# A two-layer hybrid transformer block on one core: one weight split moved by a step, the last scatter placed before the branch, and gated linear attention taken by pairs of heads

## What is computed

```python
def gla_chunked(q, k, v, glog, s0):
    g = cumsum(glog, within each chunk of 64); g_last, g_mid = ...
    att = einsum(q * exp(g - g_mid), k * exp(g_mid - g))
    att = where(tril, att, 0)
    o_intra = einsum(att, v)
    ds = einsum(k * exp(g_last - g), v); decay = exp(g_last)
    s_prev = scan over chunks: s <- decay * s + ds
    o_inter = einsum(q * exp(g), s_prev)
    return o_intra + o_inter

def gla_bidir(...):                       # both directions, summed
    return o_f + flip(o_b)

def moe_ffn(h, router, w1, w3, w2):
    combine = softmax over the 2 best experts of each token
    for e in 8 experts:
        out += combine[:, e] * ((silu(h @ w1[e]) * (h @ w3[e])) @ w2[e])
```

## Time and profile before

| | us |
|---|---|
| runs before, three | 1795.90, 1798.19, 1801.63 |
| median | 1798.19 |
| the profiled execution, its own time | 1800.37 |
| its span, first to last instruction | 1798.4 |
| TensorE busy | 1694.8 (94%) |
| VectorE busy | 1015.4 (56%) |
| ScalarE busy | 794.1 (44%) |
| data read | 404.7 MB |

### The profile page before, as it was taken

How to read it: one execution, slowest core, us unless ns; L and a number is a source line. 1 busy time by engine, 2 the same in 40 slices (tenths; PEclk the granted TensorE clock), 3 DMA queues, 4 the chain that set the end, 5 groups by cost and what they waited for, 6 DMA issues and landing times.

```text
span 1798.4 us, 25945 instructions
## 1 busy us (share of the span) xinstructions
PE 1694.8 (94%) x10337; PEld 1310.9 (73%) x10337; DVE 1015.4 (56%) x1403; ACT 794.1 (44%) x1225; POOL 55.0 (3%) x40
## 2 busy tenths in 40 slices
PE   6999989999999999999887999999999998889886
PEld 4877668988888888887677887777788887444442
DVE  3335656677677434643766986667799895101012
ACT  4416545622212223725546765556677774100101
POOL 0000000000000000000000530000000000000000
PEclk8999989999999999999978999999999999999998
DMA  8412053244467422231024977668999897899997
GB/s 332 150 71 71 1 201 145 79 185 170 185 237 263 179 94 94 80 117 48 24 71 151 357 287 258 237 235 354 344 351 360 343 360 295 327 421 421 420 421 327
DMA packets 56830, 407.53 MB, mean 227 GB/s; under 512 B 6322, under 2 KB 6450, under 8 KB 7808
## 3 DMA queue, kind: packets, MB, share of 16 engines
q1 hardware_dynamic: 56128, 404.38, 58.6%
q0 software_dynamic: 288, 0.79, 0.1%
q10 hardware_dynamic: 288, 0.63, 0.1%
HBM read 404.73 MB, written 1.05 MB: 226 GB/s over the span
## 4 chain that ended last, share of the span: by engine, by line
PE 82%; DMA 7%; DVE 5%; ACT 4%; issue 2%; SPq 0%; POOL 0%; DVEq 0%; ACTq 0%
PE psum L2243 60%; PE psum L2850 4%; DMA raw_more<-units 4%; DMA raw<-units 4%; PE psum L2860 2%; PE psum L2748 2%; PE psum L2806 1%; PE psum L2876 1%; PE psum L2888 1%; PE psum L2442 1%; PE psum L2269 1%; DVE w_lo L1551 1%; PE psum L2466 1%; PE psum L2538 1%; PE psum L2260 1%
## 5 line engine op out<-in xcount | busy, mean ns | idle before, releaser
L1551 DVE TENSOR_TENSOR w_lo<-raw,w_hi 128x1024 fp32r<-128x1024 f32 x130 | 153.0, 1220 | 144.9 <-ACT w_hi L980 144.6
L2243 PE MATMUL psum<-act_hi,w_hi 128*128 128x512 f32 (+1 forms) x608 | 221.1, 364 | 2.1 <-DVE w_lo L1551 2.1
L2243 PE MATMUL psum<-act_hi,w_lo 128*128 128x512 f32 (+1 forms) x608 | 218.7, 360 | 0.0
L2243 PE MATMUL psum<-act_lo,w_hi 128*128 128x512 f32 (+1 forms) x608 | 218.7, 360 | 0.0
L980 ACT ACTIVATE w_hi<-raw 128x1024 fp32r<-128x1024 f32 x130 | 130.3, 1053 | 161.8 <-DMA raw<-units 87.5
L2018 DVE TENSOR_TENSOR w_lo<-raw,w_hi 128x2048 fp32r<-128x2048 f32 x75 | 171.5, 2289 | 41.7 <-ACT w_hi L1360 41.4
L1360 ACT ACTIVATE w_hi<-raw 128x2048 fp32r<-128x2048 f32 x75 | 143.8, 1918 | 68.4 <-PE psum L2243 43.2
L2018 DVE TENSOR_TENSOR w_lo<-raw_more,w_hi 128x2048 fp32r<-128x2048 f32 x49 | 112.1, 2289 | 46.2 <-ACT w_hi L1360 46.0
L2243 PE MATMUL psum<-w_hi,act_hi 128*128 128x256 f32 (+1 forms) x368 | 130.2, 354 | 3.4 <-DVE w_lo L1551 1.7
L2243 PE MATMUL psum<-w_hi,xt_hi 128*128 128x512 f32 x332 | 132.1, 398 | 0.0
L2243 PE MATMUL psum<-w_lo,xt_hi 128*128 128x512 f32 x332 | 129.9, 391 | 0.0
(11 more groups left out here) (363 smaller groups left out, 3249.3 us busy)
## 6 DMA issues: line engine op xcount, KB each, us to landing
raw<-units SPq DMA_DIRECT2D x275, 1024.0 KB, 5.1
raw_more<-units SPq DMA_DIRECT2D x107, 1024.0 KB, 6.7
X<-ctx_in SPq DMA_DIRECT2D x1, 1024.0 KB, 8.5
X<-x_in SPq DMA_DIRECT2D x1, 1024.0 KB, 10.6
out<-X SPq DMA_DIRECT2D x2, 512.0 KB, 2.8
const<-const_in ACTq DMA_DIRECT2D x1, 524.0 KB, 7.4
rope<-rope_in POOLq DMA_DIRECT2D x2, 256.0 KB, 4.9
wsm<-wsm_in SPq DMA_DIRECT2D x1, 384.0 KB, 7.0
```

The costliest lines, as they stand in the source:

```text
L1551: ins = dve.tensor_tensor(w_lo[:, w_slot(i), part], raw[:, i % RING, part], w_hi[:, w_slot(i), part].bitcast(F32), ALU.subtract)
L2243: ins = pe.matmul(dst, lhs(a), rhs(b), start=first and n == 0, stop=last and n == 2)
```

## The change

Three edits.

1. The split of the last split unit (`LATE_SPLIT`, `down` of chunk 54) is taken out of `split_behind` and done by ScalarE and VectorE in step 55, behind the silu of chunk 55 and the turned columns of chunk 54.
2. TensorE's scatter of pass 7 stands before its branch (and no longer in pass 8's steps if there is one), each of the four scatters in a bank of its own with no wait for the additions before it. ScalarE's copy of the output moves behind its branch, and behind the load of the square-root table.
3. GLA goes by (pair of heads, token tile): 8 items in layer 0 and 4 in layer 1. VectorE makes two masked copies and adds the two directions into `Am_sum`; TensorE then needs one 128x128 matmul for each head where it had four of half width, and goes round the four 64x64 quadrants of its array in `M` and in the state products. `KT` and `DS` of the second pair, the scans, the products, the head sums and the splits of the output units get new places. In layer 0 the two scans are put in two items (2 and 3) and `OG` of an item stands before `DS`. In layer 1 the factors of the second pair (`gate_differences`, `gate_exps`) move forward into attention, and only one of the two output units is split by VectorE within GLA.

```diff
-SUBS_IN = {0: {4: 0, 5: 2, 16: 1}, 1: {2: 0, 3: 2, 8: 1}}
-EXPS_IN = {0: {5: 0, 6: 2}, 1: {3: 0, 4: 2}}
+SUBS_IN = {0: {4: 0, 5: 2, 16: 1}, 1: {2: 0, 3: 2, 6: 1, 7: 3}}
+EXPS_IN = {0: {5: 0, 6: 2}, 1: {3: 0, 4: 2, 7: 1, 8: 3}}
+LATE_SUBS, LATE_EXPS = {0: (3,), 1: ()}, {0: (1, 3), 1: ()}
...
+SCANS = {0: {2: (1,), 3: (3,)}, 1: {1: (1, 3)}}
...
     s = SPLIT_OF[UNIT_AT[key]] + W_RING
-    return [s] if s < split_limit(r) else []
+    return [s] if s < split_limit(r) and s != LATE_SPLIT else []
...
+LATE_SPLIT = SPLIT_OF[UNIT_AT["down", NARROW[0] * FC - 1]]
... ScalarE, gla
-                key = ("OG", l, i)
-                wait_filled(act, key)
-                act.activation(og[:, t, h * P:(h + 1) * P], bank(key)[:, 0:P], ACT.Copy)
...
+                rows_copied(2 * i + 2)
+                wait_filled(act, ("OG", l, i, 1))
+                for hh in range(2):
+                    key, h = ("OG", l, i, hh), 2 * pair + hh
+                    act.activation(og[:, t, h * P:(h + 1) * P], bank(key)[:, 0:P], ACT.Copy)
...
+                rows_copied(2 * i + 3)
... ScalarE and VectorE, run: behind the split of step g
+                if up == NARROW[0] * FC:
+                    high(LATE_SPLIT)
...
-            output(RUNS[r][-1])
...
             act.activation(std[:, 0:1], eps, ACT.Sqrt).then_inc(sem("root_table"), 1)
+            output(p)
... VectorE, gla
+            for i, (pair, t) in enumerate(gla_items(l)):
+                wait_filled(dve, ("M", l, i, 1))
...
+                for h in range(2):
+                    ins = dve.copy_predicated(Am[:, h, :, :].rearrange("p d n -> p (d n)"), tri.bitcast(I32),
+                                              bank(("M", l, i, h))[:, 0:2 * P])
...
+                empties(dve.tensor_tensor(Am_sum[:, i % 2, :, :], Am[:, :, 0, :], Am[:, :, 1, :], ALU.add), ("M", l, i, 0))
+                for dp in SCANS[l].get(i, ()):
+                    scan(l, dp)
+                for key in beside_gla(l, 2 * i) + beside_gla(l, 2 * i + 1):
+                    if key[0] == "modx":
+                        mod_step(*key)
                 if i in LOW_IN_GLA[l]:
                     split_upto(out_unit(l, LOW_IN_GLA[l][i]))
... TensorE, gla
+                for h in range(2):
+                    wait_emptied(pe, ("OG", l, i, h))
+                    pe.matmul(bank(("OG", l, i, h))[:, 0:P], Am_sum[:, i % 2, h, :], gv[:, t, (2 * pair + h) * P:(2 * pair + h + 1) * P],
+                              start=True, stop=False, skip_group_check=True)
...
+                if i < len(items):
+                    masked_scores(i)
                 if i == TURNS_AT[l]:
                     keys_turned(l, PAIR_ORDER[2:])
+                for key in beside_gla(l, 2 * i):
                     mod_step(*key)
                 if i >= 1:
+                    outputs(i - 1)
+                if i == TURNS_AT[l]:
+                    state_steps(l, PAIR_ORDER[2:])
+                for key in beside_gla(l, 2 * i + 1):
+                    mod_step(*key)
... TensorE, scatter and the end
-            before = 4 * p + (n if bank_of == SCATTER_BANK else 0)
+            before = 4 * p + (n if p != RUNS[-1][-1] and p + 1 not in RUN_STARTS else 0)
...
+            finish(RUNS[k][-1])
             with pe.If(run_valid(pe, k)):
...
-            with pe.Else():
-                finish(EXPERTS + k - 1)
```

More of the change, by code:

```diff
@@ L318 @@
 UNIT_AT = {key: m for m, key in enumerate(UNIT_LIST)}
+RUN_STARTS = tuple(passes[0] for passes in RUNS)
 RUN_END = tuple((passes[-1] + 1) * EXPERT_UNITS for passes in RUNS)
@@ L2502, in gla, with masked_scores @@
             items = gla_items(l)
+            quadrants = ((0, 0), (1, 1), (0, 1), (1, 0))
+            rows_of = lambda n: slice(n * CHUNK, (n + 1) * CHUNK)
+            def masked_scores(i):
+                pair, t = items[i]
+                pe.wait_ge(sem(f"gmul{l}"), 8 * (pair + 1))
+                for h in range(2):
+                    wait_emptied(pe, ("M", l, i, h))
+                for d in range(2):
+                    for n, (h, half) in enumerate(quadrants):
+                        r, c = rows_of(h), rows_of(2 * t + half)
+                        ins = pe.matmul(bank(("M", l, i, h))[rows_of(half), d * P + half * CHUNK:d * P + (half + 1) * CHUNK],
+                                        factors(l, 1, 2 * d + pair)[r, c], factors(l, 0, 2 * d + pair)[r, c], start=True, stop=True)
+                        if d == 1 and n >= 2:
+                            ins.then_inc(filled, 1)
```

165 lines of the change are left out of this document (75 added, 90 removed).

## The result

| | before | changed |
|---|---|---|
| median of 7 runs, us | 1801.63 | 1786.29 |
| range, us | 1795.9 to 1808.81 | 1784.65 to 1793.15 |
| ratio, with its 95% interval | 1 | 0.9918 (0.9891 to 0.9945) |
| profiled execution, us | 1800.37 | 1784.65 |
| its span, us | 1798.4 | 1782.8 |

One execution of the kernel before, beside the second group of experiments, took 3338.81 us and is left out of the ratios; all others are of one kind.

What follows compares the result with a forecast made beforehand. No single limit: DMA in the 64-slot passes, chains of short handovers at the end and in both GLAs. Terms -8.7 - 2.3 - 8.6 + 5 = -14.6 us gave a median of 1783.6, range 1774.5 to 1790.5.

Steps and rivals of the forecast that it cites:

- A, the seam: In the 64-slot passes: splitting `down` 54 one step later removes the dry DMA gap; -8.7 us (-7.5 to -9.2).
- B, the end: Behind the last `down`: scatters before TensorE's branch, ScalarE branching early, bring the last addition sooner; -2.3 us (-0.5 to -5).
- C, layer 1 with attention: Layer 1's GLA: last product starts sooner, though exponentials push attention's end by 0.7 us; -8.6 us (-4 to -10.5).
- C, layer 0: Layer 0's GLA: TensorE's work falls some 9 us, but stalls and lower clock outweigh it; +5 us (-4 to +9).
- the half clock: Layer 0's GLA: one more stretch at 1.2 GHz after the first stall, 8.8 us of work, 4.4 us lost.
- the forecast's stalls and waits: Layer 0's GLA: 3.5 us before `OG` of item 2, 3.4 at the end, 0.6 last copies, 0.4 modulation unit.
- The last stall: End of layer 0's GLA: VectorE's split and head-row scaling precede the last item's copies; TensorE stalls 3.4 us.
- R3: Layer 0's GLA: half clock lasts until the output projection; +27 us in place of +5, total 1805; chance 0.02.
- The forecast's sign of being wrong: Forecast fails if the seam still shows a dry DMA, or layer 0's first idle, some 3.5 us, is not there.
- R1: Layer 0's GLA keeps its clock and gains, -2 to +1 us; total near -20, 1778; chance 0.23.
- R4: End: ScalarE's branch hangs beyond 8 us, making it +2; total 1788; chance 0.13, with small misses up to 1790.

Runs made afterwards that it cites:

- the second group of experiments: Four kernels sharing a chip, each altering the changed kernel: layer 0 by heads, early row copy, three layer-0 moves, output by VectorE; ratios 0.9871, 0.9882, 0.9836, 0.9919.
- the three moves: Changed kernel with, in layer 0's GLA, ScalarE's row copy earlier, head sums and scans in other items, VectorE's low split last: 1774.77 us, ratio 0.9836.

## Why the prediction was right, point by point

The forecast of 1783.6 stands against 1786.29, and -14.6 against -15.3. Its terms, with the difference of the stages' means over the traces of the old and the new form:

| term | forecast | measured by stages |
|---|---|---|
| A, the seam | -8.7 (-7.5 to -9.2) | -8.8 |
| B, the end | -2.3 (-0.5 to -5) | -3.8 |
| C, layer 1 with attention | -8.6 (-4 to -10.5) | -11.6 and +2.9 ahead of it |
| C, layer 0 | +5 (-4 to +9) | +6.6 |
| sum | -14.6 | -14.7 |

**Part A** held as argued: silu 54 ran at once, the load of `down` 54 was out of everyone's way, and since loads are the limit behind it, the gap went whole.

**Part B** had the right order of events: table load, copy, scatters in one row. It was sized 1.5 us too small. The copy came 2.9 us behind the last `down`, where the forecast's terms led to scatters at 4.0 to 4.9 us (measured 3.6); and four scatters and the additions behind them took 4.6 us to the last addition where the forecast allowed 5.2. The Trainium skill's rule for a compare-and-branch (Advanced Engine Details and Errata, Control Flow Timing, about 108 ns) again did not give the price: the branch instruction took 0.05 us and the idle was 5.74. Closer is what the Trainium skill says in Runtime: NRT & Kernel Launch, Instruction fetch mechanics: a taken branch out of the current pages has to fetch its target first. The trace fits it so far: from 1761.8 to 1767.6, the time of the jump, three packets went through an instruction queue; that the jump waits for them no run shows.

**Part C, layer 1.** The chain was the one worked out, and ended 25.5 us behind the first scores by forecast and 23.2 by the trace. The copies of item 2 were done at 17.0 in place of 18.3 us, and the rest took 6.2 in place of 7.2. Ahead of it the forecast had 0.7 us in attention; the stage between the two GLAs grew by 2.9 (604.9 to 607.8 in the mean, with 2.3 us between traces of one form). Attention's share is 1.3: from layer 1's first `psum<-const,probs` matmul to its first scores it is 35.5 us in the three traces with the old layer 1 and 36.8 in all eleven with the new one. The other 1.6 lie ahead of layer 1's attention, where the changed kernel also has more half clock; no run takes them apart. The term for layer 1 came out at -8.7 against -8.6 because two errors of over 2 us, one each way, cancel.

**Part C, layer 0** had the right sign, and one term that was badly mis-sized: the half clock. Take the profiled pair, from the first scores to the og product, and count the busy time of TensorE's records at half clock half. Its work then falls from 44.7 to 34.1 us, -10.6 where the forecast had -9. Its idle time grows from 4.7 to 13.3, +8.6 where the forecast's stalls and waits (3.5, 3.4, 0.6 and 0.4) make 7.9. And 32.0 us of its work ran at half clock in place of 10.2, which costs 10.9 us more, where the forecast took one stretch more and 4.4. Together that is the +8.9 of this pair. It was four stretches, 33 us in place of 10.

The idle time was nearly right in sum and wrong in place. The last stall was forecast as 3.4 us and measured 3.58. The first was to be 3.5 us ahead of `OG` of item 2; it came as 1.72 and 1.05 us in two places. Not in the forecast at all was the growth of the first wait, for ScalarE's copy of a modulation row. Before, and then changed:

```profile
234.84 0.37 ACT L984 ACTIVATE mod_row<-psum 128x256 f32<-128x256 f32 x1
235.26 1.01 PE L2275 MATMUL psum<-const,mod_row 128*128 128x2 f32 x4 [2.36 <-ACT mod_row L984]
```

```profile
229.30 1.14 ACT L1222 ACTIVATE od_squares<-od 128x512 f32<-128x512 f32 x2
230.34 0.37 ACT L994 ACTIVATE mod_row<-psum 128x256 f32<-128x256 f32 x1
```

The copy stands behind eight exponentials and two squares, 5.2 us of work, and comes 5.6 us behind the first scores in both kernels. Before, TensorE had the outputs of a single head to do meanwhile and waited 2.36 us; now these stand behind the wait, and it is 4.13. The item-by-item working of the forecast began at 235 us, behind this wait, and so took it as it was; the 0.4 that it has for a modulation unit is far less than the 1.8 by which this wait grew. The waits for late loads grew too, from 0.36 us to 0.91 and 1.58, and one of the four half clocks came at the last of these.

R3 was the mechanism of the half clock, given 0.02 and priced at +27. The truth lay between it and the forecast: the clock came back between the stretches. The forecast's sign of being wrong ("if layer 0's first idle is not there") was met in part, with 1.05 us in place of 3.5 ahead of `OG` of item 2, and its 54 to 61 us missed the 63.4.

**The other rivals.** R1 (the clock kept, layer 0 at -2 to +1) did not occur in the changed kernel; with the three moves layer 0 gained 5.3 us against the profiled kernel before, though 16 us of it still ran at half clock. R4 did not occur: the longest jump of ScalarE in the traces was 5.88 us.

**The total** was right also by luck. Part B brought 1.5 us more than forecast and layer 0 of GLA 1.6 less, and in layer 1 two errors cancel. The profiled pair had a start that differed by 4.4 us, which no edit made; and by the ratios the kernel gained 14.8 and 12.4 us in two comparisons, each with an interval of 5 us to each side.

## What to carry to other kernels

Where a stage is a chain of handovers, less work for the fastest engine does not make it shorter by itself: follow, for every short copy that it waits for, the queue of the engine that makes it, item by item. An idle of some 2 us there may cost as much again in clock, or more. One copy moved ahead of four exponentials gained 6.6 to 8.0 us here, where the lighter matmuls by themselves had gained nothing in this layer (+6.6 us). And at the end of a program with a branch let an engine that is long through its branch do the last copy and the last stores.

## What the runs showed that was not expected

- The same instructions took 46.9 to 53.0 us to one point in 14 traces, by where the half clock fell: one of 10.2 us at 22 us cost no more than one of 3.4 us there, and one of 10.2 us at 34 us some 5 us more.
- Each engine pays for its own taken branch, ScalarE 5.4 to 5.9 us of idle, while TensorE's branch is recorded with 5.5 to 6.5 us; whichever jumps last in front of work sets the end. And loads made in advance for a pass that is not run held back the stores of the result by the queue that waits for them.
- 80 small matmuls in a row, each 30 ns apart, were followed by an idle of 3.83 us of TensorE, with no wait of the program in it. In the stretch from 226 to 236 us there one packet of 0.02 MB went through an instruction queue, at 232.6 and so within the idle, and none in the changed kernel. The Trainium skill, Runtime: NRT & Kernel Launch, Instruction fetch mechanics, has code fetched in pages while the engine executes, hidden by its slow issue; the trace fits a fetch that was not hidden, but no run tested it.
